# A two-layer decoder trunk on one core: fifty-nine matmuls on constant tiles are taken out of TensorE's program

## The chip, the core and the metric

The kernel runs on one core of one Trainium2 chip. Five engines work beside each other, each with its own instruction stream: TensorE (PE in the profile, with its weight loads as PEld), VectorE (DVE), ScalarE (ACT), GpSimd (POOL) and SyncE (SP), which here only issues transfers. They meet at semaphores. The metric is the device time of the launch in microseconds; lower is better. TensorE's clock has two levels here, 1.2 and 2.4 GHz, and the profile prints the granted share: 0.50 and 1.00.

## The reference

256 tokens of width 1024 pass two layers. Each layer has a mixer half and an expert half, in float32:

```python
mod = c_act @ ada_w[l] + ada_b[l]
shift1, scale1, gate1, shift2, scale2, gate2 = jnp.split(mod, 6, axis=-1)
h = rms_norm(x, norm1_g[l]) * (1.0 + scale1[:, None, :]) + shift1[:, None, :]
x = x + gate1[:, None, :] * hybrid_mixer(h, ...)      # h @ w_in, four mixers, gates, w_branch, w_out
h = rms_norm(x, norm2_g[l]) * (1.0 + scale2[:, None, :]) + shift2[:, None, :]
x = x + gate2[:, None, :] * grouped_moe(h, ...)       # 16 experts, top-2 inside the best group
```

The router takes sigmoid scores, picks the best group of four experts for each token, and two experts in it. Every token is sent through the experts of its group.

## The kernel before

**Tiles and precision.** A product in float32 is made of three matmuls (`exact_mm`, L632 to L636): high part by high part, low by high, high by low. Weights come from memory in units of 1 MB into a ring of six slots; ScalarE writes the high part of a unit (`early_high`, `w_high_...`), VectorE the low part (`w_low`), and TensorE multiplies. Every unit that TensorE has read frees a slot for SyncE's next transfer. The order of the work on each engine is written out by hand; semaphores hold it together.

**Start of layer 0.** TensorE waits for the first norm, turns the normed tokens (`modulate_transposes`, L680, 16 transposes), turns the small rows of parameters (L703), and sums the conditioning columns that VectorE has multiplied (`chunk_columns`, L598, matmuls with one moving column). VectorE copies these sums (`mod_sum`, L1833), forms shift and scale (`modc`), ScalarE and VectorE modulate (`hT`) and split (`h_high`, `h_low`), and the first projection starts (job "C").

**Top of layer 1.** The last expert rows are sent back (L1145), the residual is added, the norm is taken, 16 transposes follow, then modulation, split and projection.

**Second norm, router, first expert (each layer).** While token tile 1 of the output projection is added and normed by the other engines, TensorE stands in front of `turn_normed(1)` (L991, 8 transposes). Then come the router for each token tile (L1013, L1015), a fold of its parts (L1021), the counts and places of the groups (L1029 to L1034), the gathering of the normed tokens into group order (`rows0` to `rows7`, L1042, 64 matmuls), and the first expert (`dense_first`), whose first weight unit is split in four pieces (L1234 on ScalarE, L2483 on VectorE).

**The matmuls on constants.** `busy(n)` (L714 to L717) multiplies two constant tiles, the identity `ident` and the mask `future`, into bank 2, whose content nobody reads before it is overwritten. It waits for nothing of its own. It is called at eight kinds of place:

| place | calls | next instruction of TensorE waits for |
|---|---|---|
| start of layer 0 | busy(4) | the first norm |
| behind the first columns | busy(5) | shift and scale, split of `h` |
| top of layer 1 | busy(6) | last residual sum and norm |
| behind the transposes of layer 1 | busy(2) | split of `h` |
| ahead of `turn_normed(1)`, each layer | busy(7) | second norm of tile 1 |
| between the two router halves, each layer | busy(2) | split of tile 1 |
| router to counts to rows, each layer | busy(1), busy(3), busy(5) | scores, group choice, pick |
| ahead of the first expert, each layer | busy(3) | first split piece |

That is 17 matmuls in the first four rows and 21 per layer in the others: 59. A float32 matmul on plain float32 tiles shows as two records in the trace.

Of the kernel before, what the change touches and what calls it, by code (L numbers as in the profile page):

```python
# [16 lines left out]
D_MODEL, SEQ, DEPTH = 1024, 256, 2  # L17
# [151 lines left out]
def hybrid_trunk(nc, x, c, positions, ada_w, ada_b, norm1_g, w_in, q_norm_g, k_norm_g, sc_conv_w,  # L169
# [4 lines left out]
    with ctx:  # L174
        place = {}

        def sb(name, shape, dt=F32):
            place[name] = (nc.sbuf_base + 31) // 32 * 32
            return ctx.enter_context(nc.sbuf_tensor(name, [P] + shape, dt))
# [9 lines left out]
        bank = ctx.enter_context(nc.psum_tensor("bank", [P, 8, W], F32))  # L189
# [10 lines left out]
        ident = sb("ident", [P])  # L200
        tri = sb("tri", [P])
        late = sb("late", [P])
        future = sb("future", [SEQ])
# [383 lines left out]
        def _(pe):  # L587
            mm, tr = nc.tensor.matmul, nc.tensor.transpose
# [12 lines left out]
            for l in range(DEPTH):  # L601
# [6 lines left out]
                def begin(kind, name):  # L608

                    assert JOBS[kind][done[kind]] == name, (name, JOBS[kind][done[kind]])  # L610
                    pe.wait_ge(EVAC[kind], l * NJ[kind] + done[kind] + 1)
                    done[kind] += 1
                    return pj(name) if kind == "proj" else ps(name)
# [31 lines left out]
                def tok_project(out2, w, h, c0, n, hs, shared=False, tiles=range(TT), ks=range(HK)):  # L645


                    for t in tiles:
                        for k in ks:
                            last = exact_mm(out2[t], [part[:, t * P:t * P + P] for part in hs(HK * h + k)],  # L650
                                            [part[:, k, c0:c0 + n] for part in w],
                                            h == 0 and k == 0 and not (shared and t), h == 1 and k == HK - 1)
                    return last
# [45 lines left out]
                def layer_columns(layer):  # L699


                    pe.wait_ge(prow_in, (layer + 1) * (8 * 16))
                    tr(bank[:, 3, 0:PROWS], prow[0:PROWS, :], ident[0:PROWS, 0:PROWS])  # L703

                    if layer > 0:
                        pe.wait_ge(sums_ready, layer + 1)
                    for n in range(ADA_0):
                        if layer == 0 and n % 2 == 0:
                            pe.wait_ge(first_columns, n // 2 + 1)
                        c0 = (MOE_CHUNKS - ADA_0 + n) * W  # L710
                        last = chunk_columns(bank[:, 3, :], PROWS + 4 * n, ada_sums[:, c0:c0 + W])
                    last.then_inc(columns_in, 1)

                def busy(n):  # L714

                    for _ in range(n):
                        mm(bank[:, 2, 0:SEQ], ident[:, :], future[:, :], start=True, stop=True)  # L717

                if l > 0:
                    busy(6)  # L720
                    pe.wait_ge(x_tile, l * 4)
                else:
                    pe.wait_ge(first_used, 5)
                    busy(4)
                pe.wait_ge(xn_ready, l * 6 + 2)
                modulate_transposes(1)
                if l == 0:
                    layer_columns(0)
                    busy(5)
                    pe.wait_ge(pcol_ready, 2)  # L730
                else:
                    busy(2)


                b = begin("proj", "C")
# [111 lines left out]
                for i in range(4):  # L847
# [14 lines left out]
                    for u in range(2):  # L862
# [4 lines left out]
                                  stop=True, skip_group_check=True)  # L867
# [45 lines left out]
                for q in range(2):  # L913
                    b = begin("v", f"mix{q}")
                    for g in range(2):
                        for ch in range(TT):
                            last = mm(b[:, (g * TT + ch) * P:(g * TT + ch + 1) * P],
                                      gv[:, ch, (2 * q + g) * P:(2 * q + g + 1) * P], wsT[:, 2 * q + g, :],
                                      start=True, stop=True)
# [65 lines left out]
                def turn_normed(t):  # L985

                    pe.wait_ge(xn_ready, l * 6 + 4 + 2 * t)
                    for kind, q, k0 in (("s", t, 0), ("v", 2 + t, HK)):
                        b = begin(kind, f"h2_{q}")
                        for k in range(HK):  # L990
                            last = tr(b[:, k * P:k * P + P], merged[:, t, (k0 + k) * P:(k0 + k + 1) * P], ident[:, :])  # L991
                        last.then_inc(s_ready if kind == "s" else v_ready, 1)
# [1 line left out]
                tok_project(o_out[1], w1, 1, 0, W, h_late, tiles=(1,), ks=range(0, 2))  # L994
                turn_normed(0)
                tok_project(o_out[1], w1, 1, 0, W, h_late, tiles=(1,), ks=range(2, HK)).then_inc(units_read, 1)
                busy(7)
                turn_normed(1)


# [4 lines left out]
                pe.wait_ge(rw_split, 2)  # L1005
                for t in range(TT):
                    ts = slice(t * P, t * P + P)
                    if t == 1:
                        busy(2)
                    for k in range(KD):  # L1010
                        if k % HK == 0:
                            pe.wait_ge(h2_split, l * 4 + 2 * t + k // HK + 1)
                        mm(b[0:2 * NE, ts], rw_parts[:, k, :], h2_high[:, k, ts], start=k == 0, stop=False,  # L1013
                           skip_group_check=True)
                        last = mm(b[0:NE, ts], rw_parts[:, k, 0:NE], h_low[:, k, ts], start=False, stop=k == KD - 1,  # L1015
                                  skip_group_check=True)
                last.then_inc(scoresT_in, 1)
                busy(1)
                pe.wait_ge(scoresT_ready, l + 1)
                for t in range(TT):  # L1020
                    last = mm(b[:, SEQ + t * NE:SEQ + t * NE + NE], scoresT[:, t * P:t * P + P], fold[0:2 * NE, :],  # L1021
                              start=True, stop=True, skip_group_check=True)
                last.then_inc(v_ready, 1)

                b = begin("v", "count")
                busy(3)
                pe.wait_ge(gsel_ready, l + 1)
                g0, g1 = rt1[:, 5, 0, 0:EG], rt1[:, 5, 1, 0:EG]
                mm(b[:, 0:EG], ones[:, :], g0, start=True, stop=False, skip_group_check=True)  # L1029
# [3 lines left out]
                   stop=False, skip_group_check=True)  # L1033
                mm(b[:, EG:2 * EG], ones[:, :], g0, start=False, stop=True, skip_group_check=True).then_inc(v_ready, 1)  # L1034

                busy(5)
                pe.wait_ge(pick_ready, l + 1)
                pe.wait_ge(xn_split, (l + 1) * TT)
                for k in range(KD):
# [106 lines left out]
                       start=True, stop=True).then_inc(back_in, 1)  # L1146

                pe.wait_ge(proj_evac, (l + 1) * NPJ + 2)
                busy(3)
                for e in range(NE):  # L1150
                    r = e // EPG
                    if e > 0:
# [27 lines left out]
                    if r > 1 and e % EPG in (1, 2):  # L1180
                        gone, t = r - 1, e % EPG - 1
# [1445 lines left out]
```

## Time and profile before

| | |
|---|---|
| median of 3 runs | 1465.65 us (1465.24 to 1467.69) |
| the profiled execution's own time | 1466.03 us |
| its span in the trace | 1464.3 us |
| mean granted TensorE clock | 0.990 |
| TensorE busy | 1399.4 us, 96% of the span |
| VectorE busy | 1158.6 us, 79% |
| ScalarE busy | 788.2 us, 54% |
| GpSimd busy | 106.9 us, 7% |
| transfers | 357.46 MB, mean 244 GB/s |

Busy time counts the matmuls on constants too. The span leaves out 1.7 us of the execution's own time. A row of the timeline gives start, duration, engine, line, operation and shapes; what stands in square brackets is the idle time just before it and what ended that. Matmuls are pipelined, so the distance between two starts is the pace, not the duration of one.

### The profile page before, as it was taken

The numbers are of one execution on the slowest core, as the hardware profiler recorded it, in microseconds if no ns is written. First come the engines' busy times: TensorE is split into PE (matmuls) and PEld (weight loads), VectorE is DVE, ScalarE is ACT, GpSimd is POOL, SyncE is SP. The second block draws the span as 40 slices with busy tenths as digits, with TensorE's granted clock in tenths as the row PEclk, the third lists the DMA queues.
The fourth block names the chain that finished last, engine by engine and source line by source line (L and its number), as shares of the span: only waits on it lengthen the run. The fifth ranks groups of instructions, "written<-read, shape, count | busy, mean of one in ns | idle before, by whom it ended". The sixth has DMA issues, their size and how long they took to land.

```text
span 1464.3 us, 19186 instructions
## 1 busy us (share of the span) xinstructions
PE 1399.4 (96%) x7606; PEld 1129.8 (77%) x7606; DVE 1158.6 (79%) x1348; ACT 788.2 (54%) x765; POOL 106.9 (7%) x180
## 2 busy tenths in 40 slices
PE   3999899999999999999999989999999999999998
PEld 3989777788899977766578877778879997776654
DVE  7689589966788888889867886898668856799886
ACT  3567553344643466567656665534355435566673
POOL 2040012100011000000010400211000000000000
PEclk9999999999999999999999999999999999999999
DMA  9844269870678789899965532898407666899994
GB/s 348 251 145 160 71 213 312 284 267 18 230 270 315 251 287 344 312 336 373 339 185 200 168 120 86 290 288 287 169 30 287 232 200 228 295 345 351 341 370 165
DMA packets 174777, 357.46 MB, mean 244 GB/s; under 512 B 12316, under 2 KB 18704, under 8 KB 173664
## 3 DMA queue, kind: packets, MB, share of 16 engines
q1 hardware_dynamic: 161888, 310.91, 61.8%
q0 software_dynamic: 12800, 45.32, 8.8%
q8 instruction: 60, 0.98, 0.3%
q14 instruction: 29, 0.24, 0.0%
HBM read 355.16 MB, written 1.05 MB: 243 GB/s over the span
## 4 chain that ended last, share of the span: by engine, by line
PE 80%; DVE 10%; ACT 6%; issue 2%; DMA 1%; SPq 0%; DVEq 0%; ACTq 0%
PE bank L634 24%; PE bank L636 24%; PE bank L635 23%; DVE w_low L1766 4%; PE bank L1145 1%; DMA ring<-in_ada_w 1%; PE bank L598 1%; ACT w_high_zu L1249 1%; PE bank L767 1%; ACT early_high L1249 1%; PE bank L814 1%; DVE scratch L2357 1%; PE bank L1042 1%; PE bank L864 1%; ACT w_high_xbc_sc L1224 1%
## 5 line engine op out<-in xcount | busy, mean ns | idle before, releaser
L636 PE MATMUL bank<-h_high,w_low 128*128 128x256 f32 x864 | 244.1, 283 | 0.0
L1766 DVE TENSOR_TENSOR w_low<-ring,w_high_qk_score 128x2048 fp32r<-128x2048 f32 x72 | 164.7, 2288 | 37.7 <-ACT w_high_qk_score L1224 21.4
L1766 DVE TENSOR_TENSOR w_low<-ring,w_high_zu 128x2048 fp32r<-128x2048 f32 x66 | 151.0, 2289 | 43.9 <-ACT w_high_zu L1249 25.1
L635 PE MATMUL bank<-w_low,h_high 128*128 128x512 f32 (+2 forms) x480 | 182.5, 380 | 0.0
L1766 DVE TENSOR_TENSOR w_low<-ring,w_high_xbc_sc 128x2048 fp32r<-128x2048 f32 x68 | 155.6, 2288 | 28.7 <-ACT w_high_xbc_sc L1224 26.5
L636 PEld LDWEIGHTS bank<-h_high,w_low 128*128 128x128 f32 x864 | 164.0, 190 | 0.0
L635 PE MATMUL bank<-w_low,rows_high 128*128 128x512 f32 (+2 forms) x384 | 151.5, 394 | 0.0
L1224 ACT ACTIVATE w_high_zu<-ring 128x2048 fp32r<-128x2048 f32 x50 | 95.6, 1911 | 68.6 <-PE bank L636 67.0
L1224 ACT ACTIVATE w_high_xbc_sc<-ring 128x2048 fp32r<-128x2048 f32 x50 | 95.7, 1913 | 63.5 <-PE bank L636 59.6
L1224 ACT ACTIVATE w_high_qk_score<-ring 128x2048 fp32r<-128x2048 f32 x52 | 99.5, 1913 | 31.7 <-PE bank L636 29.6
L635 PEld LDWEIGHTS bank<-w_low,h_high 128*128 128x128 f32 x480 | 90.6, 189 | 18.7 <-issue 1.9
L1766 DVE TENSOR_TENSOR w_low<-ring,w_high_PT 128x2048 fp32r<-128x2048 f32 x36 | 82.3, 2286 | 5.5 <-ACT w_high_PT L1224 5.4
L1766 DVE TENSOR_TENSOR w_low<-ring,early_high 128x2048 fp32r<-128x2048 f32 (+1 forms) x27 | 58.0, 2160 | 29.7 <-ACT early_high L1249 29.6
L635 PEld LDWEIGHTS bank<-w_low,rows_high 128*128 128x128 f32 (+2 forms) x384 | 61.4, 160 | 25.7
L635 PE MATMUL bank<-w_low,hidT_high 128*128 128x512 f32 (+2 forms) x192 | 76.3, 397 | 0.0
L634 PE MATMUL bank<-h_high,early_high 128*128 128x256 f32 x256 | 74.2, 290 | 0.0
L1249 ACT ACTIVATE early_high<-ring 128x2048 fp32r<-128x2048 f32 (+1 forms) x33 | 60.1, 1828 | 24.4 <-PE bank L636 24.4
L635 PE MATMUL bank<-h_low,early_high 128*128 128x256 f32 x256 | 71.7, 280 | 0.0
L1224 ACT ACTIVATE w_high_PT<-ring 128x2048 fp32r<-128x2048 f32 x36 | 68.6, 1906 | 5.8 <-PE bank L636 4.8
L634 PE MATMUL bank<-w_high_qk_score,h_high 128*128 128x512 f32 x160 | 66.2, 414 | 3.5 <-ACT bd_qt L1554 2.2
L1249 ACT ACTIVATE w_high_qk_score<-ring 128x2048 fp32r<-128x2048 f32 x20 | 38.5, 1924 | 56.8 <-PE bank L636 56.5
L636 PE MATMUL bank<-w_high_qk_score,h_low 128*128 128x512 f32 x160 | 63.6, 397 | 0.0
(475 smaller groups left out, 3659.0 us busy)
## 6 DMA issues: line engine op xcount, KB each, us to landing
ring<-in_w_in SPq DMA_DIRECT2D x64, 1024.0 KB, 5.2
ring<-in_exp_w_up SPq DMA_DIRECT2D x64, 1024.0 KB, 5.7
ring<-in_exp_w_down SPq DMA_DIRECT2D x64, 1024.0 KB, 5.2
ring<-in_exp_w_gate SPq DMA_DIRECT2D x62, 1024.0 KB, 5.4
ada_buf<-in_ada_w POOLq DMA_DIRECT2D x40, 512.0 KB, 6.7
PT<-in_ada_w POOLq DMA_DIRECT2D x40, 512.0 KB, 7.6
ring<-in_w_branch SPq DMA_DIRECT2D x12, 1024.0 KB, 5.8
ring<-in_w_out SPq DMA_DIRECT2D x8, 1024.0 KB, 6.7
```

The costliest lines, as they stand in the source:

```text
L598: last = mm(b[:, c0 + q:c0 + q + 1], acc[:, q * P:q * P + P], ones[:, 0:1], start=True, stop=True)
L634: mm(out_, lh, rh, start=start, stop=False, skip_group_check=True)
L635: mm(out_, lh, rl, start=False, stop=False, skip_group_check=True)
L636: return mm(out_, ll, rh, start=False, stop=stop, skip_group_check=True)
L767: mm(b[:, 0:2 * ns].rearrange("p (h s) -> p h s", h=2), qiT[:, g, t * P:t * P + P], kiTd[:, 2 * u:2 * u + 2, 0:ns], start=True, stop=True) ...
L814: mm(b[:, 0:2 * ns].rearrange("p (h s) -> p h s", h=2), qT[:, i, t * P:t * P + P], kTd[:, :, 0:ns], start=True, stop=True).then_inc(v_read ...
L864: mm(b[:, u * SEQ:u * SEQ + SEQ], v_sb[:, 0, :], pt[:, 0:SEQ], start=(u == 0), stop=False, skip_group_check=True)
L1042: last = mm(b[:, 0:ROWS], part[:, t, k * P:k * P + P], pick[:, t, :], start=n == 0, stop=n == 3, skip_group_check=True)
L1145: mm(bank[:, b, :], back[0:n, r - 1, t * P:t * P + P], group_sum[0:n, j * W:j * W + W], start=True, stop=True).then_inc(back_in, 1)
L1224: A(w_high[high_at(n)][:, :, :], ring[:, n % RING, :, :], ACT.Copy).then_inc(w_rounded, 1)
L1249: A(mixer_high[n][:, :, cols], ring[:, n % RING, :, cols], ACT.Copy).then_inc(w_rounded, 1)
L1766: V.tensor_tensor(w_low[:, slot, :, cols], ring[:, slot, :, cols], high[:, :, cols], ALU.subtract).then_inc(w_split, 1)
```

## The change

The definition of `busy` and all its calls are removed. Nothing else is touched: the waits and real matmuls keep their order.

```diff
-                def busy(n):
-
-                    for _ in range(n):
-                        mm(bank[:, 2, 0:SEQ], ident[:, :], future[:, :], start=True, stop=True)
-
                 if l > 0:
-                    busy(6)
                     pe.wait_ge(x_tile, l * 4)
                 else:
                     pe.wait_ge(first_used, 5)
-                    busy(4)
                 pe.wait_ge(xn_ready, l * 6 + 2)
                 modulate_transposes(1)
                 if l == 0:
                     layer_columns(0)
-                    busy(5)
                     pe.wait_ge(pcol_ready, 2)
-                else:
-                    busy(2)
...
-                busy(7)
                 turn_normed(1)
...
-                    if t == 1:
-                        busy(2)
...
-                busy(1)
                 pe.wait_ge(scoresT_ready, l + 1)
...
-                busy(3)
                 pe.wait_ge(gsel_ready, l + 1)
...
-                busy(5)
                 pe.wait_ge(pick_ready, l + 1)
...
                 pe.wait_ge(proj_evac, (l + 1) * NPJ + 2)
-                busy(3)
                 for e in range(NE):
```

TensorE, start of layer 0, before (`scratch` holds the normed tokens, `oT_gv` the products of the conditioning columns):

```order
1 L717 MATMUL bank<-future,ident 128x256 x4
2 L680 MATMUL bank<-ident,scratch 128x128 x16
3 L703 MATMUL bank<-ident,prow 128x114
4 L598 MATMUL bank<-ones,oT_gv 128x1 x16
5 L717 MATMUL bank<-future,ident 128x256 x5
6 L634 MATMUL bank<-early_high_54,h_high 128x256
```

The same place on TensorE in the changed kernel:

```order
1 L680 MATMUL bank<-ident,scratch 128x128 x16
2 L703 MATMUL bank<-ident,prow 128x114
3 L598 MATMUL bank<-ones,oT_gv 128x1 x16
4 L634 MATMUL bank<-early_high_54,h_high 128x256
5 L635 MATMUL bank<-w_low,h_high 128x256
```

The transposes are now TensorE's first work, and nothing stands between the columns and the first projection.

TensorE, from the router's last matmul to the gathering of the rows in layer 0, before (`rt` holds the group choice, `pick` the gathering matrix):

```order
1553 L1015 MATMUL bank<-h_low,rw_parts 16x128
1554 L717 MATMUL bank<-future,ident 128x256
1555 L1021 MATMUL bank<-fold,P_sb 128x16 x2
1556 L717 MATMUL bank<-future,ident 128x256 x3
1557 L1029 MATMUL bank<-rt,ones 128x4
1558 L1030 MATMUL bank<-rt,ones 128x4
1559 L1032 MATMUL bank<-rt,tri 128x8
1560 L1034 MATMUL bank<-rt,ones 128x4
1561 L717 MATMUL bank<-future,ident 128x256 x5
1562 L1042 MATMUL bank<-pick,xn_high 128x280 x2
```

The same stretch on TensorE in the changed kernel:

```order
1549 L1002 MATMUL bank<-h_low,rw_parts 16x128
1550 L1007 MATMUL bank<-fold,P_sb 128x16 x2
1551 L1014 MATMUL bank<-rt,ones 128x4
1552 L1015 MATMUL bank<-rt,ones 128x4
1553 L1017 MATMUL bank<-rt,tri 128x8
1554 L1019 MATMUL bank<-rt,ones 128x4
1555 L1026 MATMUL bank<-pick,xn_high 128x280 x2
```

Only matmuls with few moving columns stand there now between the router and the rows.

TensorE, top of layer 1, before, and below it the changed kernel (`back` and `scratch` are the rows that are sent back, then the normed tokens):

```order
3428 L1145 MATMUL bank<-scratch,back 128x512 x4
3429 L717 MATMUL bank<-future,ident 128x256 x6
3430 L680 MATMUL bank<-ident,scratch 128x128 x16
3431 L717 MATMUL bank<-future,ident 128x256 x2
3432 L634 MATMUL bank<-early_high_54,h_high 128x256
```

```order
3420 L1129 MATMUL bank<-scratch,back 128x512 x4
3421 L680 MATMUL bank<-ident,scratch 128x128 x16
3422 L634 MATMUL bank<-early_high_54,h_high 128x256
```

The sixteen transposes are all that TensorE has between the last layer's matmuls and the next projection. On the other engines no instruction moves.

## Rows read from the trace of the kernel before

**Rows 1.** The page: busy time, share of the span, instructions; and the chain's shares.

```profile
PE 1399.4 (96%) x7606; PEld 1129.8 (77%) x7606; DVE 1158.6 (79%) x1348; ACT 788.2 (54%) x765; POOL 106.9 (7%) x180
...
PE 80%; DVE 10%; ACT 6%; issue 2%; DMA 1%; SPq 0%; DVEq 0%; ACTq 0%
```

**Rows 2.** TensorE by stretches: length, PE busy (records), granted clock, DMA share, GB/s.

```profile
152.70:155.45 2.75, 0.87 (x6) 1.00 0.95 280
155.45:162.27 6.82, 6.13 (x23) 0.50 0.11 41
...
1234.06:1237.47 3.41, 1.54 (x7) 1.00 1.05 387
1237.47:1240.88 3.41, 3.41 (x10) 0.50 0.48 184
517.30:520.70 3.40, 1.58 (x7) 1.00 1.00 378
520.70:524.10 3.40, 3.36 (x15) 1.00 0.86 321
```

**Rows 3.** Timeline of TensorE: neighbouring projection matmuls, at clock 0.50 and 1.00.

```profile
157.10 0.41 PE L635 MATMUL bank<-h_low,sc_high 128*128 128x256 f32 x1
157.31 0.41 PE L636 MATMUL bank<-h_high,w_low 128*128 128x256 f32 x1
...
163.17 0.28 PE L634 MATMUL bank<-h_high,sc_high 128*128 128x256 f32 x1
163.29 0.28 PE L635 MATMUL bank<-h_low,sc_high 128*128 128x256 f32 x1
```

**Rows 4.** Timeline, start of layer 0.

```profile
22.16 3.73 PE L717 MATMUL bank<-future,ident 128*128 128x256 f32 x8 [22.16 <-DVE oT_gv L1690]
25.81 1.97 PE L680 MATMUL bank<-ident,scratch 128*128 128x128 f32 x16
29.27 4.02 PE L598 MATMUL bank<-ones,oT_gv 128*128 128x1 f32 x32 [0.48 <-DVE oT_gv L1700]
...
37.39 0.36 PE L634 MATMUL bank<-early_high,h_high 128*128 128x256 f32 x1 [0.45 <-DVE h_low L1818]
43.69 0.39 PE L634 MATMUL bank<-early_high,h_high 128*128 128x256 f32 x1 [0.39 <-DVE w_low L1766]
```

**Rows 5.** Line 598 alone, two stretches: length, PE busy, PEld busy, clock.

```profile
29.27:32.50 3.23, 3.23 (x29) 3.23 (x29) 1.00 1.10 350
32.57:33.30 0.73, 0.72 (x4) 0.63 (x4) 0.50 1.09 345
```

**Rows 6.** Timeline of TensorE, top of layer 1.

```profile
748.03 2.75 PE L717 MATMUL bank<-future,ident 128*128 128x256 f32 x12
751.37 1.94 PE L680 MATMUL bank<-ident,scratch 128*128 128x128 f32 x16 [0.58 <-issue]
754.65 0.36 PE L634 MATMUL bank<-early_high,h_high 128*128 128x256 f32 x1 [0.47 <-DVE h_low L1818]
```

**Rows 7.** TensorE by stretches, second norm to rows, layer 0; columns as in rows 2.

```profile
365.97:366.82 0.85, 0.85 (x9) 1.00 0.00 0
369.67:370.77 1.10, 1.10 (x16) 1.00 0.00 0
371.40:371.94 0.54, 0.54 (x5) 1.00 0.00 0
374.39:374.86 0.47, 0.47 (x5) 1.00 0.00 0
378.69:382.90 4.21, 4.21 (x33) 1.00 0.74 264
```

**Rows 8.** Timeline, busy(7) and the start of the first expert, layer 0.

```profile
362.20 3.18 PE L717 MATMUL bank<-future,ident 128*128 128x256 f32 x14
...
382.96 2.54 DVE L2483 TENSOR_TENSOR w_low<-ring,w_high_xbc_sc 128x512 fp32r<-128x512 f32 x4 [1.34 <-ACT w_high_xbc_sc L1234]
384.00 0.47 PE L634 MATMUL bank<-h_high,w_high_xbc_sc 128*128 128x256 f32 x1
```

## The prediction

> **What bounds the kernel now.** I read the page first, then the granted clock by stretches, then the timeline of TensorE wherever line 717 stands. The page shows TensorE busy for 96% of the span, and the chain of waits runs 80% of its length through TensorE, 10% through VectorE, 6% through ScalarE [rows 1]. So in the projections and the experts a microsecond that TensorE loses is a microsecond of the end. The 59 removed matmuls stand elsewhere: in the few places where TensorE has nothing to do. The first question for each place is whether the real matmul behind them starts earlier without them, the second what TensorE's clock does when they are gone.
>
> For the clock, the stretches are to be compared [rows 2]. Between 152.70 and 155.45 TensorE was busy 0.87 us of 2.75, and from 155.45 to 162.27 the granted clock was 0.50, which is the 1.2 GHz level, though TensorE was busy for 6.13 us of that. Between 1234.06 and 1237.47 it was busy 1.54 of 3.41 us, and the next 3.41 us, busy throughout, stood at 0.50. But 517.30 to 520.70, busy 1.58 of 3.40 us, was followed by a stretch at 1.00. So an idle time of about two microseconds may or may not be followed by a fall, and a nearly empty 2.75 us was. What a low level costs is read from neighbouring matmuls of the same kind: 0.21 us apart at 0.50, 0.12 us apart (0.118 over a longer row of them) at 1.00 [rows 3]. Each microsecond of dense work at the low level therefore loses 1 - 0.118/0.213 = 0.45 us.
>
> **What goes and what it hid.** Except ahead of the first expert, the removed matmuls end before the awaited result is there. At the start their last record is issued before 25.81 and the transposes begin then, when the norm is ready; behind the columns, the first projection at 37.39 is released by VectorE's h_low after 0.45 us of idle time [rows 4]; at the top of layer 1 the transposes at 751.37 have 0.58 us of idle time before them and the projection at 754.65 has 0.47 us, released by h_low [rows 6]. The fourteen records from 362.20 take 3.18 us, and the transposes behind them start at 365.97, 0.6 us after they end [rows 7, 8]. So taking these away saves nothing by itself. Ahead of the first expert they end with no idle time: it starts at 384.00, while VectorE's first split piece of four (2.54 us from 382.96) is there at about 382.96 + 0.64 = 383.6 [rows 8]. Removal alone gives 0.4 us there, twice: 0.8 us. This is the whole direct gain.
>
> **Start of layer 0.** The eight records from 22.16 take 3.73 us, 0.47 us each, against 3.18/14 = 0.23 us each at 362.20 [rows 4, 8]: here TensorE starts at the low level (the profile prints no fall before its first record of the clock), and it is these matmuls that bring it up before the transposes. Without them the transposes and the columns are its first work. Sixteen transposes took 1.97 us at 1.00 [rows 4]; at half the clock about 3.5, so they end at 29.3 instead of 27.8. The columns could start at 29.27, so that costs 0.2 us or so. The columns themselves: 29 records in 3.23 us are 0.111 us each at 1.00, and the few in the low stretch stand 0.21 us apart (4 in 0.73 us with the edges) [rows 5]. All 32 at 0.21 are 6.8 us where 4.02 were taken, of which the last had already been low, plus the later start: the columns end 3.2 us later (lower end 0, if the clock comes up on the transposes; upper end 3.6, 32 times the whole difference of 0.10 and the 0.4 us). VectorE, ScalarE and the projection wait for them in a row, so the projection starts near 40.6. TensorE has by then been without work for over 4 us and begins at the low level. How long it stays low under dense work: 3.41 us in the stretch that was busy throughout, and 6.2 us of the 6.82 in the one where work resumed 0.6 us after the fall (6.13 busy) [rows 2]; the first matmuls at 22.16 needed 3.6 us until 25.81. I take the middle of 3.4 and 6.8, 5.1 us, so 5.1 x 0.45 = 2.3 us. The projection had 0.39 us of idle time before 43.69, waiting for w_low [rows 4]; that is filled now. Sum: 3.2 + 2.3 - 0.4 = 5.1 us (ends 1.1 and 6.7: 1.5 - 0.4 for a short low stretch alone, and 3.6 + 3.1).
>
> **Top of layer 1.** From 748.0 TensorE has 3.3 us without work, then 1.94 us of transposes, then 1.3 us idle, then dense work from 754.65 [rows 6]. This is emptier than each of the places in rows 2 and I expect a fall, not with certainty. If it falls, some of the transposes are late (half of 1.94 us extra, of which the modulation behind them, done quarter by quarter, passes on about 0.7) and the projection runs low for 5.1 us: 0.7 + 2.3 = 3.0 us. Ends 0 and 1.94 + 3.1 = 5.0.
>
> **Second norm to first expert, in each layer.** Without line 717 TensorE has from 362.4 to 378.69 only 0.85 us of transposes, two router halves of about 1.1 us, 0.54 us of fold and 0.9 us of counts and places; all else is idle. A fall seems certain, with no recovery before the rows. On the path: the transposes 0.85, the second router half 1.10, the fold 0.54, the counts 0.47 us, 2.96 together [rows 7]. At half clock at most 3.0 more; part of each is waiting or a pipeline's fixed end, and the transposes may still run high, so 1.6 (ends 0 and 3.0). The rows, 4.21 us dense at 1.00 [rows 7], and the experts behind them lose 5.1 x 0.45 = 2.3 us. Against that stands the gap: rows' end at 382.9 to the experts' start at 384.00 is 1.1 us, and since the rows now end after the split pieces are there, the experts follow at once and all 1.1 comes back. Sum 1.6 + 2.3 - 1.1 = 2.8 us per layer, 5.6 for two (ends per layer -0.4 and 3.0 + 3.1 - 1.1 = 5.0).
>
> Behind each place TensorE is the bound again: the waits for w_low further on are for units that VectorE splits once TensorE has freed their buffers, so they shift along and do not swallow the delay.
>
> **Sum.** 5.1 + 3.0 + 5.6 = 13.7 us on the profiled execution's own 1466.03 us gives 1479.7. That execution lies 0.38 us above the median of 1465.65, so the median to expect is 1479.3 us, 0.9% above.
>
> **A page beside it.** In the trace transposes run 0.11 to 0.12 us apart at 1.00 [rows 4, 6], and no row tells whether they alone would bring the clock up or hold it. The Trainium skill, page "TensorE: Matmul & The Clock Gate", section "Part 4: PE-mode transpose", says that transposes do not count as TensorE being busy. By that rule a fall at the top of layer 1 is certain and the transposes at the start cannot raise the clock, as my sum has it; the lower ends of those two places would drop out. On the price, the same page's terms list says that the penalty is the throttled time times (1 - K/N), half of it; the rows say 0.45 [rows 3]. With a half, the four low stretches would cost 4 x 5.1 x 0.5 = 10.2 instead of 9.2 us and the sum would be 14.7. I keep the rows' factor.
>
> **Rivals.** (a) Not slower: the clock is not lost, or only inside the idle times. For it speaks the stretch from 517.30, as empty as the one from 1234.06, with no fall behind it [rows 2]. Against it: the idle times here are 3.3 us and more against 1.8 there, and the start is at the low level anyway [rows 4]. Then only 2 x 0.4 us is gained: 1465.65 - 0.8 = 1464.9. It decides if dense work at 37.39, 754.65 and 378.69 starts at 1.00. (b) Part of it: the columns keep their pace and low stretches are short (3.41 us, 1.5 us lost each), or the top of layer 1 does not fall: start 1.1 to 3, top 0 to 1.5, norm places 1.0 each, together 3 to 6.5 us, 1470.5 in the middle. For it: the shortest low stretch is 3.41 us. (c) More: the low level holds for 10 us of dense work, 4.5 us lost, 2.2 more at each of four places, 8.8 on top: 1488. For it: nothing in the trace shows how a clock recovers after more than 4 us without work except the start, where 3.6 us did; so it is unlikely. (d) The change does nothing at one kind of place because TensorE isn't first to be waited for there; that is part of (b).
>
> **Chances and range.** Forecast 68%, (b) 16%, (c) 8%, (a) 8%. The forecast's own spread: each of four low stretches between 3.4 and 6.8 us is +-0.8 us, which adds to about +-2, the delays on the path +-2: 1475 to 1484. To leave out no more than 2 in 10, the range takes in the upper part of (b) and the lower of (c): 1470.5 to 1486. Within 0.2% (2.9 us) of the old time is what a measurement of this kernel cannot tell from no change: (a) falls there with 7 of its 8 points; faster by more than that 1%; slower 92%.
>
> **What the changed profile would show.** The transposes at the start spaced at 0.21 us and the columns taking 6.5 us or more instead of 4.02; the first projection starting near 40.6 rather than 37.39; granted clock 0.50 in 3.4 to 6.8 us of dense work at four places: the first projection of each layer and the rows with the first expert of each layer; no idle time between rows and expert; elsewhere the same distances. Mean granted clock near 0.97. It would be wrong if the rows (64 records) keep 4.2 us, if the start of the projection stays at 37.4, or if the delay at one of these places is gone a hundred microseconds later because a wait there got shorter.

## The result: 0.28% slower, a third of the forecast

| kernel | median | lowest to highest | runs |
|---|---|---|---|
| before | 1466.98 us | 1463.39 to 1469.26 | 22 |
| changed | 1471.32 us | 1466.51 to 1475.90 | 22 |

The ratio is 1.0028, with a 95% interval of 1.0016 to 1.0040: 4.3 us slower where 13.7 were forecast. Nine further times of the changed kernel, taken later, had a median of 1475.38 (ratio 1.0042, 1.0025 to 1.0059). The direction was right, the size was not, and the spread of the changed kernel (9.4 us against 5.9) was not foreseen: its 31 times form a group at 1466.5 to 1467.9 (8 runs), a group at 1475.2 to 1476.0 (11 runs) and a dozen between. All ratios here are of executions in the same, faster state; one time of a variant below, 1982.4 us at a mean granted clock of 0.652, is outside it and is counted in no ratio.

The page of the changed kernel, engines and chain, as in [rows 1]. This execution took 1467.54 us, its span is 1465.8:

```profile
PE 1378.9 (94%) x7488; PEld 1117.8 (76%) x7488; DVE 1158.5 (79%) x1348; ACT 788.5 (54%) x765; POOL 106.9 (7%) x180
...
PE 81%; DVE 9%; ACT 6%; issue 2%; DMA 1%; SPq 0%; DVEq 0%; ACTq 0%
```

118 records fewer, 20.5 us less busy time, and nothing gained: TensorE's share of the chain is 81% where it was 80%. Five of the ten stretches of the same trace at the low level, as in [rows 2] (length, PE busy and records, granted clock, DMA share, GB/s):

```profile
33.61:40.44 6.83, 2.84 (x13) 0.50 1.13 284
364.70:371.53 6.83, 5.33 (x40) 0.50 0.00 1
374.94:385.18 10.24, 7.54 (x32) 0.50 0.51 165
753.82:757.24 3.42, 3.02 (x15) 0.50 0.57 118
...
1088.33:1101.98 13.65, 8.53 (x36) 0.50 0.38 135
```

The clock does fall at all four places that the prediction named (the stretches at 364.70 and 374.94 both lie in the norm place of layer 0). The mean granted clock went from 0.990 to 0.980 (0.97 was forecast). What the falls cost is read below by comparing the start of each real matmul with its start in the trace of before: the delay. TensorE executes the same 7488 real records in both, so each has a partner. Two traces of before differ by up to 0.5 us in such a delay at the start, where nothing is edited.

### The profile page after: what moved, and what is told of

It reads as the page before. It is cut to its first block, busy times and chain, and to the rows that moved or that the text cites. A ratio compares the mean times of both kernels' runs of the same rounds, so it can differ in the third digit from the quotient of the medians.

```text
span 1465.8 us, 18954 instructions
## 1 busy us (share of the span) xinstructions
PE 1378.9 (94%) x7488; PEld 1117.8 (76%) x7488; DVE 1158.5 (79%) x1348; ACT 788.5 (54%) x765; POOL 106.9 (7%) x180
## 3 DMA queue, kind: packets, MB, share of 16 engines
HBM read 355.16 MB, written 1.05 MB: 243 GB/s over the span
## 4 chain that ended last, share of the span: by engine, by line
PE 81%; DVE 9%; ACT 6%; issue 2%; DMA 1%; SPq 0%; DVEq 0%; ACTq 0%
PE bank L634 24%; PE bank L636 24%; PE bank L635 24%; DVE w_low L1749 4%; PE bank L1129 1%; DMA ring<-in_ada_w 1%; PE bank L598 1%; PE bank L1026 1%; ACT w_high_zu L1232 1%; PE bank L757 1%; PE bank L804 1%; DVE scratch L2340 1%; PE bank L854 1%; ACT w_high_xbc_sc L1207 1%; ACT P_sb L1440 1%
## 5 line engine op out<-in xcount | busy, mean ns | idle before, releaser
L634 PE MATMUL bank<-early_high,h_high 128*128 128x512 f32 (+2 forms) x160 | 60.2, 376 | 4.5 <-DVE h_low L1801 4.5
```

The source lines that it names most:

```text
L634: mm(out_, lh, rh, start=start, stop=False, skip_group_check=True)
```

## The experiments

Each ratio below is to times of the kernel before that were taken beside it; their medians lie between 1466.3 and 1467.1 us.

### The changed kernel again: the start has two courses

> The changed kernel once more, nothing edited, for a second trace and more times. Its 22 times so far lie between 1466.5 and 1475.9 us, wider than the 1463.4 to 1469.3 of before, and its trace belongs to one of the shortest (1467.5). Theory 1 (the moments at which the clock falls and rises lie differently against the program in each run): this trace shows the low stretches at other moments than the first, the first projection may start up to 3 us later than 37.6 because the 32 column matmuls run low, and the delay at each place, traced matmul by matmul against before, is different; median 1468 to 1474. Theory 2 (a difference that has nothing to do with the clock, such as late transfers): the low stretches lie as in the first trace and the difference, if any, shows as waits for ring transfers.

Median 1475.38 us of 9 runs (1468.24 to 1475.96); the traced execution has a span of 1473.8 us. TensorE's timeline at the start, first the changed kernel's first trace, then this one (start, duration, engine, line, operation, idle time before):

```profile
25.91 3.65 PE L680 MATMUL bank<-ident,scratch 128*128 128x128 f32 x16 [25.91 <-ACT scratch L1285]
...
29.54 3.96 PE L598 MATMUL bank<-ones,oT_gv 128*128 128x1 f32 x32
37.60 0.55 PE L634 MATMUL bank<-early_high,h_high 128*128 128x256 f32 x1 [4.10 <-DVE h_low L1801]
```

```profile
25.95 3.65 PE L680 MATMUL bank<-ident,scratch 128*128 128x128 f32 x16 [25.95 <-ACT scratch L1285]
...
29.59 6.85 PE L598 MATMUL bank<-ones,oT_gv 128*128 128x1 f32 x32
40.53 0.55 PE L634 MATMUL bank<-early_high,h_high 128*128 128x256 f32 x1 [4.10 <-DVE h_low L1801]
```

In both the transposes run at the low level, 3.65 us instead of the 1.97 of [rows 4], and the delay is 0.3 us when the columns start, because before the columns had 0.48 us of idle time in front of them, waiting for VectorE [rows 4]. Then the courses part. In the first trace the clock rises at 30.20 and the 32 column records keep their pace (3.96 us). In the second they take 6.85 us, all of them low, and the projection starts 3.1 us later than before. A little behind it, at the matmul that stood at 44.14 before, the delay is 0.86 us in the first trace and 4.51 in the second. Theory 1 holds: it is the same program with other moments of fall and rise. The traced executions took 1467.54 and 1475.61 us, one from each group of times; whether the upper group is the late course throughout is not shown, since only these two were traced. The rest of the difference between these two traces comes at falls scattered through the span that one has and the other has not: two behind one-column matmuls near 1008 and 1045, for instance, which together added 3.1 us in the second. Over all traces such a fall of 3.41 us within dense work (near 285, 320, 521, 606, 1004 or 1042) adds 1.5 to 1.6 us wherever it lies, which is the 0.45 us per us of the prediction.

### Each place put back alone

Start of layer 0 only:

```diff
 (the changed kernel)
                     pe.wait_ge(first_used, 5)
+                    busy(4)
...
                     layer_columns(0)
+                    busy(5)
```

> The changed kernel with the matmuls on constants put back at the start of layer 0 alone (4 ahead of the transposes, 5 behind the columns). If the start carries most of the loss (prediction: 5.1 of 13.7 us): 3 to 5 us below the changed kernel, 1467 to 1468. If the start costs about the 1 us that the first trace shows: 0.5 to 1.5 us below it, 1470 to 1471. In either case the first projection starts near 37.4 and runs at clock 1.00.

Second norm, router, first expert, both layers, only:

```diff
 (the changed kernel)
+                busy(7)
                 turn_normed(1)
...
+                    if t == 1:
+                        busy(2)
...
+                busy(1)
...
+                busy(3)
...
+                busy(5)
...
+                busy(3)
                 for e in range(NE):
```

> The changed kernel with the matmuls on constants put back at the second norm, the router and the first expert of both layers (21 in each), none elsewhere. The first trace shows 2.0 and 1.8 us of delay behind these two places, the prediction said 2.8 each. Theory 1: 3 to 5 us below the changed kernel, 1466 to 1468, with the 64 row matmuls back at 4.2 us. If these places cost nothing on the median: the same as the changed kernel.

Top of layer 1 only:

```diff
 (the changed kernel)
                 if l > 0:
+                    busy(6)
...
+                else:
+                    busy(2)
```

> The changed kernel with the matmuls on constants put back at the top of layer 1 alone (6 and 2). Prediction: 3.0 us are lost there; then this lies 3 us below the changed kernel, 1468. The first trace shows no loss there once the wait for the low part of the first unit is passed (delay 1.9 us ahead of it, 1.6 behind it): then no difference, within 1 us.

Medians 1468.76, 1471.41 and 1471.40 us; ratios to before 1.0012 (1.0001 to 1.0022), 1.0030 (1.0020 to 1.0040) and 1.0028 (1.0018 to 1.0039). So with the start restored 1.8 us of loss are left, and with either of the others 4.1 to 4.4. The start is the largest single part. The changed kernel's own times beside these three had the ratio 1.0042, so against them the norm places and the top give back 1.8 and 2.1 us, within intervals that overlap; medians of 9 and 12 runs over a spread of 5 us are a blunt measure. One thing is clearer: the group at 1475 and above, 11 of the 31 times of the changed kernel, is in none of these three, nor in any later variant of it (none above 1473.2 us, but for the one named above). Why each of them removes it stays open. Two expectations were missed: with the norm places back 1466 to 1468 was expected, and with the start back the projection was to begin near 37.4 at 1.00. In that trace it began at 38.36, since the clock rose only at 28.2 and was low again from 31.63 to 38.46.

The delays gained at each place, in the traces that lack the matmuls there (us, against the first trace of before; "start" at the matmul of 44.14, "norm" from 361.7 to 392.9 and from 1077.5 to 1100.6, "top" from 745.0 to 763.3):

| trace | start | norm, layer 0 | top of layer 1 | norm, layer 1 |
|---|---|---|---|---|
| changed | 0.86 | 2.34 | 0.00 | 1.65 |
| changed, again | 4.51 | 1.92 | 0.47 | 1.61 |
| start put back | (0.98) | 1.90 | 0.16 | 2.20 |
| norm put back | 4.89 | (0.00) | 0.71 | (0.00) |
| top put back | 2.30 | 2.31 | (0.01) | 1.62 |
| forecast | 5.1 | 2.8 | 3.0 | 2.8 |

Brackets mark a place where the matmuls stand. The zeros of the norm places with them, and the 1.6 to 2.3 us without, show that the loss belongs to them. Behind the place of layer 0, 0.5 us of it is made up again by 515 us in the four traces that lack the matmuls there. In layer 1 nothing is.

### Can transposes raise the clock?

Ahead of the transposes of layer 0 in the changed kernel, four matmuls on constants, or sixteen transposes of the identity:

```diff
 (the changed kernel, first try)
                     pe.wait_ge(first_used, 5)
+                    for _ in range(4):
+                        mm(bank[:, 2, 0:SEQ], ident[:, :], future[:, :], start=True, stop=True)
```

> The changed kernel with the four matmuls on constants put back ahead of the transposes of layer 0, nothing else. Two traces of the changed kernel differ at the start: in one the clock rises at 30.2 us, the 32 column records keep 0.11 us and the first projection starts at 37.6; in the other it rises at 45.0, they take 0.21 us and it starts at 40.9. Theory 1: the four matmuls decide between the two. Then no run has the late start: columns at 0.11 us, projection at 37.4 to 37.6, times without the upper group (1475), median 1468 to 1470. Rival: the five matmuls behind the columns matter as much; then times stay spread up to 1475.

```diff
 (the changed kernel, second try)
                     pe.wait_ge(first_used, 5)
+                    for q in range(16):
+                        tr(bank[:, 2, (q % 4) * P:(q % 4) * P + P], ident[:, :], ident[:, :])
```

> As the last, but sixteen transposes of the identity (128 moving columns each, into the same unread bank) stand in place of the four matmuls on constants, about as long at the low level. If transposes raise the clock as matmuls do: same as the kernel with the four matmuls, clock at 1.00 near 26 to 28 us, projection at 37.4 to 37.6, no times near 1475. If transposes do not count as work for the clock (the rule of the Trainium skill that the prediction weighed): as without them, late start in about half the runs, median 1470 or more.

Medians 1471.54 us of 8 (the time of 1982.4 us is one of them; 1471.52 without it) and 1468.77 us, ratios 1.0028 (1.0017 to 1.0039) and 1.0016 (1.0006 to 1.0027). Timeline of the start with the sixteen extra transposes (L719):

```profile
22.23 3.65 PE L719 MATMUL bank<-ident 128*128 128x128 f32 x16 [22.23 <-DVE oT_gv L1675]
25.89 3.08 PE L680 MATMUL bank<-ident,scratch 128*128 128x128 f32 x16
...
29.34 4.94 PE L598 MATMUL bank<-ones,oT_gv 128*128 128x1 f32 x32 [0.28 <-DVE oT_gv L1685]
```

The clock rose at 28.2 us in this trace, when 27 of the 32 transposes had started and TensorE had executed nothing else. The kernel with both groups of constant matmuls restored rose at the same 28.2 in its trace and shows nearly the same rows:

```profile
22.22 3.75 PE L717 MATMUL bank<-future,ident 128*128 128x256 f32 x8 [22.22 <-DVE oT_gv L1680]
25.88 3.09 PE L680 MATMUL bank<-ident,scratch 128*128 128x128 f32 x16
...
29.34 4.92 PE L598 MATMUL bank<-ones,oT_gv 128*128 128x1 f32 x32 [0.27 <-DVE oT_gv L1690]
```

So transposes do raise this clock, as matmuls do. The rule that the prediction set beside its sum, that transposes do not count as TensorE being busy (the Trainium skill, "TensorE: Matmul & The Clock Gate", "Part 4: PE-mode transpose"), fails here: the rise at 28.2 us contradicts it. Over all traces: the eight with work ahead of the transposes (both of before and six variants) have the first rise between 25.7 and 28.2 us and columns of 3.7 to 5.4 us. The six without have it at 28.98, 30.09 and 30.20 in three, and at 44.8, 45.0 and 45.5 in the other three. So work ahead of the transposes decides between the two courses, as far as these fourteen traces show. The times show less of it: with the four alone the ratio is 1.0028, that of the changed kernel's first set, and lower only than that of its second (1.0042). My expectation of 1468 to 1470 was missed. With the sixteen transposes the projection started at 38.38, later than the 37.4 to 37.6 that was expected, because the clock fell again at 31.6.

### The five behind the columns alone, and the five ahead of the rows alone

```diff
 (the changed kernel)
                     layer_columns(0)
+                    for _ in range(5):
+                        mm(bank[:, 2, 0:SEQ], ident[:, :], future[:, :], start=True, stop=True)
                     pe.wait_ge(pcol_ready, 2)
```

> The changed kernel with the five matmuls on constants put back behind the columns only. With the start's two shares apart: the four ahead of the transposes decide the columns (late start 3 us in part of the runs), the five decide the low stretch in the first projection (0.5 to 2.3 us). Theory: the columns still run low in part of the runs (upper group stays, projection near 41), but where the clock is up at the columns the projection runs at 1.00: median 1469 to 1474, lowest about 1 us below that of the changed kernel. Rival: the five also need the clock up, stretch to 4.3 us at the low level and delay the projection by themselves.

Median 1469.89 us, ratio 1.0021 (1.0012 to 1.0029). Its trace is one with the early rise; the projection then starts with a delay of 0.51 us and still has 0.52 at the matmul of 44.14, where the changed kernel's early-rise trace goes from 0.21 to 0.86. The lowest time, 1467.02, is no lower than without them, and the upper group that was expected to stay is gone (highest 1472.70).

```diff
 (the changed kernel, each layer)
+                for _ in range(5):
+                    mm(bank[:, 2, 0:SEQ], ident[:, :], future[:, :], start=True, stop=True)
                 pe.wait_ge(pick_ready, l + 1)
```

> The changed kernel with only the five matmuls on constants ahead of the rows of each layer put back. In three traces of the changed kernel the place from second norm to first expert delays by 0.8 to 1.2 us ahead of the rows and by 2.6 more in the rows at the low level, of which 1.1 comes back. If the five bring the clock up in time: the rows keep 4.2 us, the delay per layer falls from about 2.0 to 1.0, and the time lies 2 us below the changed kernel. Rival: they run at the low level themselves, 0.44 us a record, so ten records last 4.4 us instead of 2.2, end after the pick is ready (3.4 us behind their start) and delay the rows by 1 us: no gain.

Median 1468.58 us, ratio 1.0011 (1.0000 to 1.0022). The trace shows both theories at work. TensorE's timeline, the five (L1022) and the rows (L1028), and below it the rows (L1026) of the changed kernel without them:

```profile
382.48 4.21 PE L1022 MATMUL bank<-future,ident 128*128 128x256 f32 x10
386.34 0.61 PE L1028 MATMUL bank<-pick,xn_high 128*128 128x280 f32 x2
386.79 0.42 PE L1028 MATMUL bank<-pick,xn_low 128*128 128x280 f32 x2
```

```profile
379.48 0.83 PE L1026 MATMUL bank<-pick,xn_high 128*128 128x280 f32 x2 [2.36 <-DVE pick L2450]
380.11 0.67 PE L1026 MATMUL bank<-pick,xn_low 128*128 128x280 f32 x2
380.58 0.67 PE L1026 MATMUL bank<-pick,xn_high 128*128 128x280 f32 x2
```

The ten records run low, overshoot the pick and start the rows 1.4 us later than in the changed kernel, by delay; but they bring the clock up, the pairs of rows then stand 0.26 us apart and not 0.47, and over the whole place the delay is 1.2 and 1.0 us instead of 1.6 to 2.3. So they gain 0.4 to 1.2 us per layer in the traces, although they end too late.

### Before again, and more matmuls on constants

> The kernel before once more, for a second trace of it. Theory 1 (the moments of the fall shift against the program from run to run): the same three kinds of places as in its first trace (after the transposes near 155 and 872, behind one-column matmuls near 284, 320, 606, 1001, 1037, and near 1237), but not the same members fall; the time stays between 1463 and 1470. Rival: always the same members fall.

1466.42 us. Falls at 32.6, 155.5, 606.1, 872.3 and 1237.5 again, one new at 520.7 (behind the idle time after which the clock had stayed up, [rows 2]), none at 319.3. So some falls belong to the kernel before too, and not all of them return.

```diff
 (the kernel before)
                         b_scb = begin("proj", "scb")
+                        busy(5)
...
                         if e == DENSE:
                             pe.wait_ge(rows_ready, l + 1)
+                            for _ in range(4):
+                                mm(bank[:, 0, 0:SEQ], ident[:, :], future[:, :], start=True, stop=True)
```

> The kernel before with more matmuls on constants: five ahead of the first half of scb in each layer, where TensorE idles 2.46 us and the clock then stood at 0.50 for 6.8 us, and four ahead of the first rows of expert 4, where it idles 1.87 us. If the fall is what these idle times cost (3.1 us per layer at the first place by 0.45 x 6.8): 3 to 6 us below before, 1460 to 1463, no low stretch at 155 and 872. If the added matmuls only delay what follows, or the stretches ahead of scb keep falling: same as before or 1 us slower.

Median 1471.27 us, ratio 1.0023 (1.0013 to 1.0033): slower. The trace says why:

```profile
156.05 3.81 PE L717 MATMUL bank<-future,ident 128*128 128x256 f32 x10 [2.46 <-DVE xbc L2070]
159.51 0.47 PE L634 MATMUL bank<-h_high,sc_high 128*128 128x256 f32 x1
```

The idle time was a wait for the bank, which `begin` makes, so the five stood behind it and only delayed. The four stood where there was no idle time; they delayed what follows by 1.7 us, and the idle time behind them gave all of it back. The rest of that trace's loss is the five (1.1 and 1.3 us) and scattered falls. Moved ahead of the waits:

```diff
 (the kernel before)
                     if i == 0:
+                        for _ in range(5):
+                            mm(ps("ab00")[:, 0:SEQ], ident[:, :], future[:, :], start=True, stop=True)
                         b_scb = begin("proj", "scb")
...
+                        if e == DENSE:
+                            busy(4)
                         for h in range(2):
                             rows_half(2, up_unit(e), h, r)
```

> The kernel before with five matmuls on constants ahead of the wait for the bank of scb (written to the bank of ab00, free there), and four ahead of the up product of expert 4, where TensorE idles 1.87 us. In the last try they stood behind the wait for the bank and ahead of the wrong product: the trace showed the five start at 156.05, when the idle time was over, and the four where there was none. If idle time without work is what lets the clock fall there: the five run from 153.6 to 155.8, the delay behind scb is gone, no low stretch near 155 and 872, and 2 to 5 us less than before, 1462 to 1465. If falls near 155 go on (the idle 1.0 us ahead of the transposes is enough): same as before.

Median 1463.21 us (1458.78 to 1466.77, 11 runs), ratio 0.9979 (0.9968 to 0.9990). In its trace the five (L856) fill the gap, the projection behind them starts as soon as VectorE frees the bank, and the stretch that stood at 0.50 in [rows 2] is at 1.00:

```profile
153.38 2.33 PE L856 MATMUL bank<-future,ident 128*128 128x256 f32 x10
156.01 0.38 PE L634 MATMUL bank<-h_high,sc_high 128*128 128x256 f32 x1 [0.30 <-DVE xbc L2071]
```

```profile
151.40:155.45 4.05, 3.02 (x19) 1.00 0.63 202
155.45:162.27 6.82, 5.99 (x44) 1.00 0.10 36
```

That is 2.5 us ahead of before by 176 us, and 2.5 more at the same place of layer 1. At the four TensorE's lead stays the same in layer 0 and grows by 1.6 us in layer 1, where the fall at 1237.47 of [rows 2] is missing; but that fall is missing without the four too, as is shown below, so no gain of theirs is shown. Last, the same kernel without the three matmuls ahead of the first expert:

```diff
 (the kernel of the last experiment)
                 pe.wait_ge(proj_evac, (l + 1) * NPJ + 2)
-                busy(3)
                 for e in range(NE):
```

> The kernel that beat before (five matmuls on constants ahead of scb's bank, four ahead of expert 4's up product), now without the three ahead of the first expert of each layer. The prediction gave this removal as the only direct gain, 0.4 us per layer, because VectorE's first split piece is there 0.4 us before the three end. If so: the first expert starts 0.4 us nearer to the rows than the 1.1 us of before, at clock 1.00 as before, 0.8 us in all, too little for the times: same as the kernel with them, 1462 to 1464. Rival: the clock falls behind the rows without them and 1 to 2 us are lost per layer.

Median 1462.23 us (1457.98 to 1466.44, 12 runs), ratio 0.9966 (0.9950 to 0.9982). Between 361.7 and 392.9 the delay falls by 0.36 us, at the place in layer 1 by 0.77: the direct gain that the prediction put at 0.4 each. The clock did not fall there. In layer 0 a wait for VectorE's `w_low` at 394.46 takes 0.3 us of it back.

```profile
379.90 0.42 PE L1044 MATMUL bank<-pick,xn_low 128*128 128x280 f32 x2
381.02 0.36 PE L634 MATMUL bank<-h_high,w_high_xbc_sc 128*128 128x256 f32 x1 [0.70 <-DVE w_low L2486]
```

The first expert now waits for the split piece, with 0.70 us of idle time. This is the fastest kernel of the study; whether it beats the one with the three is within the spread. One of the times of before beside it, 1475.88 us, lies 7 us above the others; without it the ratio would be 0.9970.

## Why the prediction was wrong, step by step

The mechanism, low clock in the dense work behind emptied idle times, was right at the start and at the norm places, where the terms were too large. It failed at the top of layer 1, where in the two traces of the changed kernel 1 us of dense work or none ran low, and the falls elsewhere were left out of the sum. In size the result is that of rival (b), 3 to 6.5 us, which had 16%. That is in part luck: (b) had 1.0 us for each norm place, where the traces show 1.9, and it does not name the falls that pulled the total down.

- **What bounds the kernel, and that removal saves nothing: right.** The transposes start at 25.91 against 25.81, `turn_normed(1)` waits for ScalarE's `scratch` with the matmuls and without them, and the direct gain was 0.36 and 0.77 us against 0.4 each.
- **Price of low dense work, 0.45 us per us: right.** In the rows of layer 0, low from 379.48 on, the delay grew from 0.80 to 3.27 us by 385.01, which is 0.45 per us.
- **Start of layer 0, 5.1 us: right in half of the traces.** The step that failed is "the transposes and the columns are its first work", and so low from the first transpose to the last column. The transposes can bring the clock up, in time for the columns. Three of six traces have the late course (4.5 to 4.9 us, as forecast, projection at 40.5 in the second trace where 40.6 was said), three the early one (0.5 to 2.3). The mean of the six is 2.9. Rival (b) named the early course, with 1.1 to 3 us. The recorded 3.2 us for the columns is also 0.2 more than its own terms give (6.8 - 4.02 + 0.2 = 3.0).
- **Top of layer 1, 3.0 us: wrong, 0.0 to 0.7.** The clock falls, but the step "the projection runs low for 5.1 us" does not follow. In the second trace the low stretch is used up by the waiting time and the transposes before the projection starts:

```profile
758.40:761.81 3.41, 3.32 (x17) 0.50 0.66 84
```

```profile
758.13 3.40 PE L680 MATMUL bank<-ident,scratch 128*128 128x128 f32 x16 [3.17 <-issue]
761.62 0.46 PE L634 MATMUL bank<-early_high,h_high 128*128 128x256 f32 x1
```

  The last transposes were 1.3 us later there than ahead of the place, yet the projection only 0.2: the 0.47 us of idle time before it in [rows 6] shrank to 0.09, and the engines between took up the rest. In the first trace the low stretch reached into the projection and cost 0.4 us, which came back at the wait for the low part of the next unit (0.38 us of idle time before, none after): the delay is 1.64 us ahead of the place and 1.64 behind it. The prediction held that such waits do not swallow a delay.
- **Second norm to first expert, 2.8 us per layer: mis-sized, 1.6 to 2.3, mean 1.9.** The term of 1.6 us for the path ahead of the rows was 0.4 to 1.1. In the first trace, layer 0, the first router half ended 1.5 us late, but the second began only 0.5 late, because it waits for h_low; the fold passed on the 1.0 us that the second half had by its end; and of the 1.8 us at the end of the counts the rows kept 1.05. The rows and the experts lost 0.6 to 1.3 net, where the sum had 2.3 - 1.1 = 1.2. In the first trace the clock rose at 371.53 and fell again at 374.94: "no recovery before the rows" was wrong too, though the rows ran low all the same.
- **The sum.** 2.9 + 0.3 + 2 x 1.9 = 7.0 us by the traces instead of 13.7. The two sets of times say 0.28% and 0.42%, 4.1 and 6.2 us. Part of the gap comes from falls outside the four places. At 155 both traces of before stand low for 6.8 us and both of the changed kernel for 3.4: between 150.9 and 276.7 the delay shrinks by 1.1 and 0.75 us. The fall at 1237.47 in [rows 2] is in both traces of before and in none of the twelve others, and the delay drops there by 1.6 us in each of them. In the changed kernel the same idle time is there and no fall comes behind it:

```profile
1237.13:1240.54 3.41, 1.55 (x7) 1.00 1.01 350
1240.54:1243.96 3.42, 3.42 (x17) 1.00 0.52 191
```

  In the first trace the four places add 4.8 us, these two falls take off 2.7, and another 0.5 comes back between 392.9 and 515: it ends 1.5 us behind before. The second ends 9.6 us behind, with three scattered falls more than before. I did not count such falls because the change does not touch them; yet where they lie differs from run to run. Whether the missing fall at 1237 follows from the change, and how much of the median all this makes, stays open.

## What to carry to other kernels

Idle time of TensorE is priced by what follows it: dense work behind it runs at the low clock and loses 0.45 us per us, while a low stretch that lies over waits and transposes cost 0.0 to 0.7 us at the top of layer 1. Matmuls on constants pay in full if they are over when the awaited result comes (the five ahead of the rows overshot it by 1.4 us and kept only part of their gain), and so should stand ahead of every wait of the idle time, the wait for the bank too: the same five cost 0.23% behind it (with four more in a wrong place) and gained 0.21% ahead of it (with four more whose share is not shown). When one trace is read for clock effects, take a second of the same program: here two traces differed by 8 us with nothing edited.

## What was not expected of the hardware

- Transposes alone raised TensorE's clock (first rise at 28.2 us, with 27 of 32 started and no other matmul ahead of them).
- One-column float32 matmuls scale with the clock like wide ones: 32 records took 3.96 us at 1.00 (mostly) and 6.85 at 0.50.
- The profile prints 1.00 for the granted clock before its first record of a change, though the pace there is that of the low level: the 6.85 us of columns above lie in a stretch printed as 1.00.

```profile
29.59:36.44 6.85, 6.84 (x34) 1.00 1.13 316
```
